# A two-part transformer kernel on one core: another order in its opening stage, context rows scaled on GpSimd, and waits for a quarter of a weight unit

## The chip, the cores and the metric

The kernel runs on 1 core of one Trainium2 chip. The metric is device time in microseconds (us), lower is better. TensorE does the matrix products, VectorE (DVE), ScalarE (ACT) and GpSimd (POOL) the element-wise work, SyncE (SP) issues most transfers.

## The reference

512 tokens `x` and 256 context tokens `ctx`, both 1024 wide, pass through two modulated layers, and `x` then through a larger block. For this change it is enough to see how a layer begins:

```python
mod_x = (silu_c @ w_mod[i] + b_mod[i])[:, None, :]
mod_c = silu_cc @ w_mod[i] + b_mod[i]
sh_x, sc_x, g_x = jnp.split(mod_x, 3, axis=-1)
sh_c, sc_c, g_c = jnp.split(mod_c, 3, axis=-1)
hx = rms_norm(x, norm_g[i]) * (1.0 + sc_x) + sh_x
hc = rms_norm(ctx, norm_g[i]) * (1.0 + sc_c) + sh_c
# layer 0 (a): grouped attention with rotary positions over x and ctx
q, k, v, z = cut(hx @ w_in); kc, vc = cut(hc @ w_in)   # and qc, zc
...
# layer 1 (b): attention in a neighbourhood, and to the context
```

So nothing of a layer can be projected before its row norms and its modulation vectors (shift, scale and gate, each 1024 wide, for `x` and for `ctx`) are there. All data are float32.

## The kernel before

**Layout.** Tokens lie along the free dimension, features over the 128 partitions in 8 chunks k. `XX` holds x (8 x 512 columns), `XC` the context (8 x 256). A float32 product is made of three matmuls on parts in a shorter format: high part `WH` by high part `HX`, `WH` by the rest `LX` of the activations, rest `WL` of the weights by `HX` (L1267 to L1269; L1262 to L1264 where tokens are the stationary side; `HC` and `LC` are the context's parts).

**Weights** come in 1 MB units (`UNITS`), 128 x 2048 each, two buffers deep (`load`). A unit is split into its parts in four quarters of 512 columns: ScalarE casts a quarter to `WH` (L1549), then GpSimd, or VectorE for the first two units and in `flush`, subtracts it to `WL` (L2255, L1800). `tick` puts the next quarter into the plan, between chunks of projections. Chunk k of a unit lies in quarter k // 2. `proj` waits at k = 0 for all four quarters (L1254, L1255).

**Modulation units** are split in nothing: 16 small matmuls (`mod_mm`, L1280), ScalarE copies the sums to a row (`mod_row`, L1556), TensorE turns it into columns (`mod_tr`, L1289), VectorE adds the bias (L1806). Unit i of a layer holds shift (i from 0 to 3), scale (4 to 7) or gate (8 to 11) of chunks 2i and 2i + 1, modulo 8. Six of layer 0's units (`EARLY`) have buffers of their own, four of them; units 2 and 6 come through the ordinary stream.

**Opening stage.** First loads: vectors, x in two halves, context, then early units on SP's queue; the constants `C` and the rotary table `CS` on ScalarE's queue. Squares of x and ctx, added up chunk by chunk (L1566, L1568, L1814), column sums on TensorE (`norm_sums`, L1298), the power -1/2 on GpSimd (`norm_rs`, L2261), and six diagonal products that spread it over PSUM (`rbroad`, L1305). Then `modulate` per chunk k: VectorE multiplies x by gain and norm (`scale`, L1856), ScalarE adds the shift and casts to `HX` (L1576), VectorE makes the rest `LX` (`scale_low`, L1863); the context part of the chunk the same way just behind, on the same engines. `keys_rows` projects the keys of chunk k as chunks come free. Next come the values (`values`), the norm and rotation of the keys (`a_key_sums`, `a_key_norm`, `a_key_rope`), the first pair of queries (`gen_aq(0)`: `a_query_raw`, `a_query_sums`, `a_query_rope`), and the first scores of attention (L1347).

**Order.** The program is one list (`plan`) that each engine walks in the order in which `do` was called, taking the steps that it has a part in. An engine that waits in a step holds up all its later steps. Banks of PSUM are given out by rings.

Of the kernel before, what the change touches and what calls it, by code (L numbers as in the profile page):

```python
# [74 lines left out]
EARLY = [0, 4, 1, 5, 3, 7]  # L75
# [91 lines left out]
def build(nc, wu, vp, cc, cs1, xt, biasb, pos, out):  # L167
    ctx = ExitStack()
    with ctx:
# [81 lines left out]
        s_gain, s_scaled, s_res = signal("mod_gain"), signal("scaled"), signal("residual")  # L251
        s_r2 = signal("norm2")
# [161 lines left out]
        def early_load(n):  # L414
            do("early", n)

        def early_unit(n, nxt=None):
            w = early[n % 4].rearrange("p (k f) -> p k f", k=8)
            run(mod_unit(0, EARLY[n], MODS, w, (s_early[n % 4], (n,)), lambda: early_load(nxt) if nxt else None))

# [36 lines left out]

        part_by = {}
        scaled = {}

        def modulate(l, Rb, rb, perm, hb, phase, first):
            a = smc(16).rearrange("p (f j) -> p f j", j=2)
            scaled[l] = (a, Rb, rb, perm, hb, phase, first)
            for k in range(KC):
                do("scale", l, k)
                for j in range(2):
                    part_by[phase, k, j] = "dve"
                if k:
                    do("scale_low", l, k - 1)
                if k == KC - 1:  # L470
                    do("scale_low", l, k)
                yield k
# [7 lines left out]
        partsrc = {}  # L480
        WIDE = ring((0, 1), (2, 3), (4, 5), (6, 7))
# [9 lines left out]
        mod = [smc(48).rearrange("p (f j) -> p f j", j=2) for _ in range(2)]  # L491
        do("first_loads")
# [7 lines left out]
        do("silu")  # L500
        for n in range(2):
            split(n)
        ar = Arena()
        hb0 = Rows(ar(4096), ar(2048))
        norm("a", ar, 6, (), lambda k: [(s_x[k // 4], (k // 4,)), (s_x[2], (2,))])
        for k in range(KC):
            do("square", "a", k)
        early_unit(0, 4)
        early_unit(1, 5)
        close("a", MODS)  # L510
        WIDE.take("RA", (s_scaled, (0, 7, 1)))
        RbA = PS[:, 0:1024]
        rbroad("a", 6, RbA)
        mods = modulate(0, RbA, "a", False, hb0, "a", ())
        next(mods), next(mods)
        un = Unit("ak")

# [7 lines left out]
        early_unit(2)  # L525
        early_unit(3)
        keys_rows([0])
# [3 lines left out]
        keys_rows([1, 2])  # L531
        unv = Unit("av")
        run(mod_units(0, (2,), MODS))
        run(mod_units(0, (6,), MODS))
        next(mods), next(mods)
        keys_rows([3, 4])
        early_unit(4)
        early_unit(5)
        next(mods), next(mods)
        keys_rows([5, 6, 7])  # L540
# [12 lines left out]
        ksq, krr = [tmpS, PbA[0]], [PTbA[0], PTbA[1]]  # L553
        kss = smc(24)
# [9 lines left out]
        values((0, 1))  # L564
        do("a_key_sums")
        values((2, 3))
        for m in range(2):
            do("a_key_norm", m)
        values((4,))
        for m in range(2):  # L570
            do("a_key_rope", m)
        values((5,))
        unv.done(s_proj, "av", 5)
        for b in range(4, 8):
            last[b] = [(s_ksin, ((b - 4) // 2,))]

# [185 lines left out]
        run(gen_aq(0, FA))  # L762
# [45 lines left out]
        b0 = WIDE.take("RB", (s_scaled, (1, 7, 1)))  # L808
# [17 lines left out]

        def b_free(a):

            return [(s_post, ("b", 8 * (a - 2) + 7))] if a >= 2 else [(s_xl_dve, ("b", 7, 1))]
# [419 lines left out]
        def tensor(e, w):  # L1249
            def proj(g, k):  # L1250
                G = groups[g]
                if k == 0:
                    free(w, g)
                    for q in range(4):  # L1254
                        w.wait_ge(*w_low(G.unit, q))  # L1255
# [36 lines left out]
            def norm_sums(name):  # L1292
# [3 lines left out]
                w.wait_ge(*s_acc(name, 7))  # L1296
# [31 lines left out]
            def a_query_sums(pair):  # L1328
                free(w, ("aqs", pair))
                w.wait_ge(*s_qsq(pair, 1))  # L1330
                for i in range(6):
                    t = e.matmul(aqps[pair, "sums"][:, 2 * i:2 * i + 2], tmpS[:, i * 128:i * 128 + 128], c("ind"), start=True, stop=True)
# [52 lines left out]
            def m_gates():  # L1385
                free(w, "gw")
                for q in range(4):
                    w.wait_ge(*w_low(gwu, q))
                part = PART[gwu]
                for k in range(8):  # L1390
                    w.wait_ge(*x_low("h", k, 0))
# [140 lines left out]
        def scalar(e, w):  # L1532
            def first_loads():
                e.dma_start(C[:, :], cc).then_inc(*s_c.by())

            def rope_load():
                e.dma_start(CS[:, :], cs1).then_inc(*s_cs.by())

# [18 lines left out]

            def square(name, k):
# [11 lines left out]

            def scale(l, k):
                a, Rb, rb, perm, hb, phase, first = scaled[l]
                for j, (lo, hi) in enumerate(FULL):
                    w.wait_ge(*s_scaled(l, k, j))
                    await_all(w, first)
                    e.activation(H.at(k, lo, hi), hb.at(k, lo, hi), ACT.Identity, bias=mod[l][:, k, j:j + 1]).then_inc(*s_xh.by(phase, k, j))  # L1576
# [7 lines left out]
            def a_key_raw(m):  # L1584
                w.wait_ge(*s_proj("ak", 1, 1))
                w.wait_ge(*s_xl_dve("a", 7, 1))
# [9 lines left out]
            def a_query_raw(pair, j):  # L1596
                lo, hi = FULL[j]
                w.wait_ge(*s_proj("aq", pair, j))
                await_all(w, [(s_qrope, (pair - 1,))] if pair else [(s_krope, (0,)), (s_krope, (1,))])
                e.activation(tmpS[:, lo:hi], groups["aq", pair, j].out[:, 0:hi - lo], ACT.Square).then_inc(*s_qsq.by(pair, j))  # L1600
# [972 lines left out]
```

## Time and profile before

| | |
|---|---|
| median of 3 runs | 1780.09 us (1779.31 to 1780.92) |
| the profiled execution | 1784.24 us, its span 1782.5 us |
| TensorE busy | 1607.6 us, 90% |
| VectorE, ScalarE, GpSimd busy | 732.4, 611.6, 606.9 us |
| granted TensorE clock, mean | 0.941 of full speed |

Busy time is the sum of instructions' durations. Rows of a timeline begin with start and duration (us), and in brackets at the end the engine's idle time before the instruction and what ended it. In the rows PE is TensorE's matmuls and PEld its weight loads.

### The profile page before, as it was taken

To read this page: it belongs to the slowest core of one execution; us is meant where nothing else is said; L and a number is where in the kernel's file an instruction comes from. 1 tells how busy PE (TensorE), PEld (TensorE's weight loads), DVE (VectorE), ACT (ScalarE), POOL (GpSimd) and SP (SyncE) were. 2 spreads that over 40 slices of the span, in tenths; PEclk is the share of its full clock that TensorE was granted. 3 is DMA by queue.
4 is the path that set the end of the run, shared out by engine and by line. 5 is a ranking of instruction groups with operands and counts; after the bars stand their busy time and mean duration, and the time that the engine had idled before them with its cause. 6 is when DMAs were issued, how large, how long until landed. Compare 5 with 4: busy or idle time off the path is not lost.

```text
span 1782.5 us, 25034 instructions
## 1 busy us (share of the span) xinstructions
PE 1607.6 (90%) x9858; PEld 1255.4 (70%) x9858; DVE 732.4 (41%) x1730; ACT 611.6 (34%) x1289; POOL 606.9 (34%) x590
## 2 busy tenths in 40 slices
PE   3799999999869799999997879999999888999987
PEld 2577777777648688788876658778787775555756
DVE  3434444444442524345355452514332354554033
ACT  3224444434432323333334342424332233333221
POOL 0033334333222124243333443435345233332351
PEclk9789999999969899999999989999999899999998
DMA  7201011111222222121221202122121211111221
GB/s 309 80 24 48 35 41 49 44 48 49 87 101 92 100 72 83 65 87 57 89 71 48 95 30 94 48 71 79 63 94 48 95 71 43 53 48 48 71 89 53
DMA packets 22148, 128.21 MB, mean 72 GB/s; under 512 B 2448, under 2 KB 2576, under 8 KB 8080
## 3 DMA queue, kind: packets, MB, share of 16 engines
q1 hardware_dynamic: 21600, 125.03, 19.5%
q8 instruction: 79, 1.29, 0.3%
q10 hardware_dynamic: 432, 1.58, 0.2%
q14 instruction: 37, 0.30, 0.0%
HBM read 124.50 MB, written 2.10 MB: 71 GB/s over the span
## 4 chain that ended last, share of the span: by engine, by line
PE 75%; DVE 10%; issue 5%; POOL 4%; ACT 4%; DMA 2%; SPq 0%; DVEq 0%; POOLq 0%; ACTq 0%
PE PS L1267 14%; PE PS L1268 13%; PE PS L1269 13%; PE PS L1347 6%; PE PS L1382 6%; PE PS L1357 5%; PE PS L1513 3%; PE PS L1262 2%; PE PS L1263 2%; PE PS L1264 2%; POOL WL L2255 2%; DVE sm L1940 1%; PE PS L1523 1%; DVE AR L2054 1%; DVE AR L1856 1%
## 5 line engine op out<-in xcount | busy, mean ns | idle before, releaser
L2255 POOL TENSOR_TENSOR WL<-W,WH 128x512 fp32r<-128x512 f32 x268 | 348.0, 1313 | 475.9 <-ACT WH L1549 475.4
L1267 PE MATMUL PS<-HX,WH 128*128 128x512 f32 x1008 | 421.1, 418 | 38.4 <-POOL WL L2255 18.3
L1268 PE MATMUL PS<-LX,WH 128*128 128x512 f32 x1008 | 403.8, 401 | 0.0
L1269 PE MATMUL PS<-HX,WL 128*128 128x512 f32 x1008 | 403.4, 400 | 0.0
L1267 PEld LDWEIGHTS PS<-HX,WH 128*128 128x128 f32 x1008 | 196.5, 195 | 88.8 <-issue 30.5
L1269 PEld LDWEIGHTS PS<-HX,WL 128*128 128x128 f32 x1008 | 195.5, 194 | 43.3
L1268 PEld LDWEIGHTS PS<-LX,WH 128*128 128x128 f32 x1008 | 196.6, 195 | 37.3 <-issue 1.7
L1549 ACT CAST WH<-W 128x512 fp32r<-128x512 f32 x296 | 170.8, 616 | 42.0 <-DMA W<-in_wu 34.7
L1618 ACT ACTIVATE AR<-PS,sm 128x768 f32<-128x768 f32 (+4 forms) x160 | 115.5, 722 | 182.5 <-DVE sm L1945 105.3
L1940 DVE TENSOR_REDUCE sm<-PS 128x1 f32<-128x512 f32 (+4 forms) x224 | 149.9, 669 | 43.7 <-PE PS L1347 39.3
L2298 POOL TENSOR_SCALAR AR<-AR,sm 128x768 f32<-128x768 f32 (+1 forms) x96 | 73.3, 763 | 231.3 <-DVE sm L1956 231.3
L1347 PE MATMUL PS<-AR 64*128 64x256 f32 (+3 forms) x704 | 128.1, 472 | 13.7 <-ACT XC L1618 5.2
L1382 PE MATMUL PS<-AR 128*64 128x128 f32 x1408 | 102.6, 294 | 20.7 <-DVE AR L1965 12.0
L1382 PEld LDWEIGHTS PS<-AR 128*64 128x64 f32 x1408 | 81.8, 145 | 49.1 <-issue 31.0
L1347 PEld LDWEIGHTS PS<-AR 64*128 64x128 f32 x704 | 61.5, 191 | 68.4 <-issue 45.8
L1262 PE MATMUL PS<-WH,HX 128*128 128x256 f32 x320 | 95.6, 299 | 14.7 <-POOL WL L2255 14.7
L1357 PE MATMUL PS<-C,AR 128*128 128x128 f32 x608 | 103.9, 291 | 4.4 <-DVE AR L1976 4.1
L1628 ACT COPY AR<-PS 128x512 f32<-128x512 f32 (+1 forms) x112 | 62.1, 554 | 126.4 <-PE PS L1357 125.9
L2298 POOL TENSOR_SCALAR XC<-XC,sm 128x512 f32<-128x512 f32 x64 | 44.7, 698 | 162.9 <-DVE sm L1956 162.9
L1357 PEld LDWEIGHTS PS<-C,AR 128*128 128x128 f32 x608 | 71.3, 146 | 40.6 <-issue 25.4
L1618 ACT ACTIVATE XC<-PS,sm 128x512 f32<-128x512 f32 x64 | 44.1, 690 | 150.6 <-DVE sm L1945 150.6
L1263 PE MATMUL PS<-WH,LX 128*128 128x256 f32 x320 | 93.3, 292 | 0.0
(266 smaller groups left out, 2467.7 us busy)
## 6 DMA issues: line engine op xcount, KB each, us to landing
W<-in_wu SPq DMA_DIRECT2D x100, 1024.0 KB, 4.8
AR<-in_biasb SPq DMA_DIRECT2D x32, 256.0 KB, 2.6
AR<-in_wu SPq DMA_DIRECT2D x6, 1024.0 KB, 15.4
XX<-in_xt SPq DMA_DIRECT2D x2, 1024.0 KB, 9.7
out<-XX SPq DMA_DIRECT2D x8, 256.0 KB, 2.2
XC<-in_xt SPq DMA_DIRECT2D x1, 1024.0 KB, 12.7
C<-in_cc ACTq DMA_DIRECT2D x1, 770.5 KB, 5.3
CS<-in_cs ACTq DMA_DIRECT2D x1, 512.0 KB, 8.8
```

The source lines that it names most:

```text
L1262: e.matmul(o, xh, wh, start=(k == 0), stop=False)
L1263: e.matmul(o, xl, wh, start=False, stop=False)
L1267: e.matmul(o, wh, xh, start=(k == 0), stop=False)
L1268: e.matmul(o, wh, xl, start=False, stop=False)
L1269: t = e.matmul(o, wl, xh, start=False, stop=(k == 7))
L1347: t = e.matmul(PS[:, s.score[h] + a:s.score[h] + b], l, r, start=True, stop=True)
L1357: t = e.transpose(o[:, j * 128:j * 128 + 128], s.pb[h][:, (q0 + j) * 128:(q0 + j) * 128 + 128], c("id"))
L1382: t = e.matmul(s.out[h], s.values[h][j], s.pt[h][:, j * 128:j * 128 + 128], start=(j == 0 and s.first), stop=(j == nv - 1 and s.final))
L1549: e.copy(WH[:, PART[n], a:z], W[:, n % 2, a:z]).then_inc(*s_wh.by(n, q))
L1618: e.activation(s.pb[h][:, 0:s.n], PS[:, s.score[h]:s.score[h] + s.n], ACT.Exp, bias=smn[:, i % 4:i % 4 + 1], scale=(1.0 if s.scale is None ...
L1940: e.tensor_reduce(mx, x, AX.X, ALU.max).then_inc(*s_max.by(name, n, h))
L2255: e.tensor_tensor(WL[:, d, a:z], W[:, n % 2, a:z], WH[:, d, a:z].bitcast(F32), ALU.subtract).then_inc(*s_wl_pool.by(n, q))
```

## The change

In the opening stage:

- The constants go onto SP's queue behind the context, and the rotary table behind the second weight unit. All eight shift and scale units of layer 0 are `EARLY` ones (units 2 and 6 leave the stream); units 4 to 7 of them wait in SP's queue for the four buffers.
- The squares are made and added for x first, by halves as they land, then for the context.
- `norm_sums` goes between the first and the second `mod_mm`, the first `mod_tr` behind the second, the second behind `rbroad`. Later modulation units go in pairs, both `mod_mm` ahead of both `mod_tr`, with a chunk of key projections between.
- The first query pair is projected between the values, with a scratch tile of its own.

In both layers' `modulate` the context's part moves: ScalarE copies the context's norms to SBUF (`Rc`), GpSimd multiplies all eight chunks by them, then per chunk multiplies by the gain and adds the shift; ScalarE only casts, and GpSimd makes the rest `LC`.

In the whole kernel `proj` waits for quarter k // 2 at chunk k in place of all four at k = 0, and `m_gates` likewise. Waits for the last context part go to GpSimd's signal (`H_A`, `H_B`).

```diff
-    u = [("ak",), ("av",), ("mod", 0, 2), ("mod", 0, 6), ("aqz", 0)]
+    u = [("ak",), ("av",), ("aqz", 0)]
-EARLY = [0, 4, 1, 5, 3, 7]
+EARLY = [0, 4, 1, 5, 2, 6, 3, 7]
...
         def modulate(l, Rb, rb, perm, hb, phase, first):
+            do("scale_ctx", l)
             for k in range(KC):
                 do("scale", l, k)
-                for j in range(2):
-                    part_by[phase, k, j] = "dve"
+                part_by[phase, k, 0], part_by[phase, k, 1] = "dve", "pool"
...
         do("first_loads")
-        for n in range(2):
-            early_load(n)
+        do("early", range(4))
         load(0)
-        for n in range(2, 4):
-            early_load(n)
+        do("early", range(4, 8))
         load(1)
         do("rope_load")
         do("silu")
...
+        for j in range(2):
+            for k in range(KC):
+                do("square_part", "a", k, j)
+        first = [early_unit(n, FIRST if n < 4 else MODS) for n in range(8)]
+        next(first[0])
+        norm_sums("a", FIRST)
+        next(first[1])
+        run(first[0])
+        do("norm_rs", "a")
...
+        rbroad("a", 6, RbA)
+        run(first[1])
+        for n in range(2):
+            split(n)
         mods = modulate(0, RbA, "a", False, hb0, "a", ())
-        next(mods), next(mods)
+        next(mods)
         un = Unit("ak")
+        next(mods)
+        next(first[2])
+        next(first[3])
+        run(first[2])
+        run(first[3])
...
+        for n in (4, 6):
+            next(mods), next(mods)
+            keys_rows([n - 4])
+            next(first[n])
+            next(first[n + 1])
+            keys_rows([n - 3])
+            run(first[n])
+            run(first[n + 1])
         next(mods), next(mods)
         while pieces:
             tick()
         unv = Unit("av")
-        keys_rows([5, 6, 7])
+        keys_rows([4, 5, 6, 7])
...
-        run(gen_aq(0, FA))
+        aq0 = gen_aq(0, vr)
...
+        values((0, 1))
+        key_work[0]()
+        values((2,))
+        key_work[1]()
+        to_pause(aq0), to_pause(aq0)
+        key_work[2]()
+        values((3,))
+        to_pause(aq0)
+        values((4,))
+        run(aq0)
+        values((5,))
...
# TensorE, proj
                 if k == 0:
                     free(w, g)
-                    for q in range(4):
-                        w.wait_ge(*w_low(G.unit, q))
+                w.wait_ge(*w_low(G.unit, k // 2))
...
# ScalarE
+            def scale_ctx(l):
...
+                w.wait_ge(*s_rb(rb, 5))
...
+                e.copy(Rc, Rb[:, T:NT]).then_inc(*s_rc.by(l))
             def scale(l, k):
+                w.wait_ge(*s_scaled(l, k))
+                e.activation(H.at(k, 0, T), hb.at(k, 0, T), ACT.Identity, bias=mod[l][:, k, 0:1]).then_inc(*s_xh.by(phase, k, 0))
+                w.wait_ge(*s_scaled_ctx(l, k))
+                e.copy(H.at(k, T, NT), hb.at(k, T, NT)).then_inc(*s_xh.by(phase, k, 1))
...
# GpSimd
+            def scale_ctx(l):
+                w.wait_ge(*s_rc(l))
...
+                for k in range(KC):
+                    e.tensor_tensor(hb.at(k, T, NT), xT.at(k, T, NT), Rc, ALU.mult).then_inc(*s_normed_ctx.by(l, k))
+            def scale(l, k):
...
+                w.wait_ge(*s_gain(l, k | 1))
+                w.wait_ge(*s_normed_ctx(l, k))
+                e.tensor_scalar(hb.at(k, T, NT), hb.at(k, T, NT), a[:, k, 1:2], mod[l][:, k, 1:2], ALU.mult, ALU.add).then_inc(*s_scaled_ctx.by(l, k))
+            def scale_low(l, k):
...
+                w.wait_ge(*s_xh(phase, k, 1))
+                e.tensor_tensor(L.at(k, T, NT), hb.at(k, T, NT), H.at(k, T, NT).bitcast(F32), ALU.subtract).then_inc(*s_xl_pool.by(phase, k, 1))
...
# SyncE
+                e.dma_start(C[:, :], cc).then_inc(*s_c.by())
...
+            def early_(ns):
+                for n in ns:
+                    if n >= 4:
+                        w.wait_ge(*s_modmm(0, EARLY[n - 4]))
+                    e.dma_start(early[n % 4], wu[len(UNITS) + n]).then_inc(*s_early[n % 4].by(n))
```

The comment lines that name an engine are added here. `key_work` is the list of `a_key_sums`, `a_key_norm` and `a_key_rope`; `to_pause` runs the query generator to its next pause: x's projection, the context's, `a_query_sums`, then `a_query_rope` with the rest.

## Rows read from the trace of the kernel before

**Rows 1.** Busy time by stretch: length, then each engine, granted clock, DMA share, GB/s

```profile
0.00:45.06 45.06, 16.77 (x104) 11.21 (x105) 14.97 (x30) 14.27 (x30) 1.86 (x7) 0.95 0.78 310
45.06:88.50 43.44, 33.06 (x177) 24.72 (x178) 18.29 (x41) 10.29 (x20) 0.00 (x0) 0.70 0.21 77
88.50:130.20 41.70, 37.96 (x284) 33.89 (x283) 12.97 (x20) 13.54 (x19) 17.76 (x11) 0.90 0.07 26
130.20:136.00 5.80, 5.79 (x15) 3.61 (x16) 2.41 (x5) 1.58 (x3) 0.23 (x1) 0.51 0.01 3
...
606.50:632.50 26.00, 18.22 (x72) 14.35 (x73) 23.45 (x43) 11.64 (x21) 0.00 (x0) 0.86 0.15 53
```

**Rows 2.** Waits of TensorE: total us, times, longest

```profile
PE PS L1267 <- POOL WL L2255: 18.3, 10, 4.1
PE PS L1262 <- POOL WL L2255: 14.7, 5, 5.5
```

**Rows 3.** Timeline of the opening stage, TensorE

```profile
17.38 1.93 PE L1280 MATMUL PS<-AR,sm 128*32 128x256 f32 x16 [17.38 <-DMA AR<-in_wu]
...
27.58 2.70 PE L1298 MATMUL PS<-C,AR 128*128 128x1 f32 x12
32.33 2.93 PE L1305 MATMUL PS<-AR,C 128*128 128x128 f32 x12 [2.05 <-DVE AR L1836]
...
40.79 0.98 PE L1289 MATMUL PS<-C,AR 128*128 128x2 f32 x4 [3.71 <-ACT AR L1556]
...
45.06 0.77 PE L1267 MATMUL PS<-HX,WH 128*128 128x512 f32 x1
...
130.21 2.93 PE L1347 MATMUL PS<-AR 64*128 64x512 f32 x8 [3.10 <-DVE AR L1914]
```

**Rows 4.** Timeline of the opening stage, ScalarE and VectorE

```profile
14.93 0.63 ACT L1566 ACTIVATE AR<-XX 128x512 f32<-128x512 f32 x1 [9.30 <-DMA XC<-in_xt]
...
16.72 7.33 DVE L1814 TENSOR_TENSOR AR<-AR 128x768 f32<-128x768 f32 x7 [10.88 <-ACT AR L1568]
...
38.22 2.16 ACT L1549 CAST WH<-W 128x512 fp32r<-128x512 f32 x4
```

**Rows 5.** Busy time by stretch, the transfers at full rate (last column GB/s)

```profile
10.00:20.00 10.00, 1.93 (x16) 0.59 (x16) 2.96 (x4) 4.62 (x11) 0.00 (x0) 1.00 1.01 423
```

**Rows 6.** Groups by shape, GpSimd: count, busy us, mean ns, idle before

```profile
L2272 POOL TENSOR_TENSOR LC<-AR,HC 128x256 fp32r<-128x256 f32 x4 | 4.2, 1056 | 0.0
L2298 POOL TENSOR_SCALAR AR<-AR,sm 128x256 f32<-128x256 f32 x32 | 15.3, 478 | 54.1 <-DVE sm L1956 54.1
L2276 POOL TENSOR_TENSOR sm<-sm 128x24 f32<-128x24 f32 x1 | 4.2, 4162 | 3.9 <-DVE sm L1882 3.9
```

**Rows 7.** Busy time by stretch: key projections first, then a stretch of values, then queries

```profile
45.06:50.33 5.27, 5.27 (x17) 4.40 (x17) 4.80 (x11) 2.65 (x5) 0.00 (x0) 0.50 0.08 33
...
98.40:101.50 3.10, 3.10 (x17) 3.10 (x16) 0.32 (x1) 0.00 (x0) 3.10 (x2) 0.50 0.00 0
115.00:120.40 5.40, 5.40 (x24) 4.46 (x25) 0.86 (x2) 5.30 (x8) 0.00 (x0) 1.00 0.00 0
```

**Rows 8.** Timeline: three of TensorE's 15 waits for quarters, and one pair of quarters

```profile
930.43 0.47 PE L1267 MATMUL PS<-HX,WH 128*128 128x512 f32 x1 [4.09 <-POOL WL L2255]
...
1065.80 2.56 POOL L2255 TENSOR_TENSOR WL<-W,WH 128x512 fp32r<-128x512 f32 x2 [6.44 <-ACT WH L1549]
...
1068.50 0.55 PE L1262 MATMUL PS<-WH,HX 128*128 128x256 f32 x1 [5.52 <-POOL WL L2255]
...
1719.64 0.72 PE L1267 MATMUL PS<-HX,WH 128*128 128x512 f32 x1 [2.89 <-POOL WL L2255]
```

**Rows 9.** Timeline, GpSimd and VectorE at work on SBUF together

```profile
111.11 2.53 POOL L2281 TENSOR_TENSOR AR<-AR,CS 128x512 f32<-128x512 f32 x2 [7.15 <-PE PS L1326]
...
112.50 1.70 DVE L1894 TENSOR_TENSOR AR<-AR 128x512 f32<-128x512 f32 x1 [0.74 <-POOL AR L2281]
114.83 0.69 DVE L1894 TENSOR_TENSOR AR<-AR 128x512 f32<-128x512 f32 x1
```

More of the change, by code:

```diff
@@ L412, in mod_units, with early_unit @@
                 yield from mod_unit(l, u, pr, unit_w(un.n), (s_w[un.n % 2], (un.n,)), lambda: un.done(s_modmm, l, u))
-        def early_load(n):
-            do("early", n)
-        def early_unit(n, nxt=None):
+        def early_unit(n, pr):
             w = early[n % 4].rearrange("p (k f) -> p k f", k=8)
-            run(mod_unit(0, EARLY[n], MODS, w, (s_early[n % 4], (n,)), lambda: early_load(nxt) if nxt else None))
+            return mod_unit(0, EARLY[n], pr, w, (s_early[n % 4], (n,)), lambda: None)
         @dataclass
@@ L500, in build @@
         do("silu")
+        ar = Arena()
+        hb0 = Rows(ar(4096), ar(2048))
+        norm("a", ar, 6, (), None)
+        for j in range(2):
[7 more added lines that the diff above has]
+        do("norm_rs", "a")
+        WIDE.take("RA", (s_scaled, (0, 7)), (s_rc, (0,)))
+        RbA = PS[:, 0:1024]
+        rbroad("a", 6, RbA)
+        run(first[1])
         for n in range(2):
             split(n)
[L503 to L513, printed above, removed]
         mods = modulate(0, RbA, "a", False, hb0, "a", ())
-        next(mods), next(mods)
+        next(mods)
         un = Unit("ak")
+        next(mods)
[3 more added lines that the diff above has]
+        run(first[3])
         def keys_rows(ks):
@@ L553, in build @@
         ksq, krr = [tmpS, PbA[0]], [PTbA[0], PTbA[1]]
+        qtmp = [PbA[1] if pair == 0 else tmpS for pair in range(8)]
         kss = smc(24)
@@ L563, in values @@
                 do("a_value", s)
[L564 to L573, printed above, removed]
         for b in range(4, 8):
             last[b] = [(s_ksin, ((b - 4) // 2,))]
+        key_work = [lambda: do("a_key_sums"), lambda: [do("a_key_norm", m) for m in range(2)], lambda: [do("a_key_rope", m) for m in range(2)]]
         @dataclass
@@ L761, in fill_a, with to_pause @@
             yield from parts_a(range(7))
-        run(gen_aq(0, FA))
+        aq0 = gen_aq(0, vr)
+        def to_pause(g):
+            while next(g) != PAUSE:
+                pass
+        values((0, 1))
[9 more added lines that the diff above has]
+        values((5,))
+        unv.done(s_proj, "av", 5)
         attention("a", [s for pair in range(8) for s in steps_a(pair)], SA, TA, PbA, PTbA, OA, fill_a(), 8 * 15 * (T + LC) / 100 + 14 * 5, posted_a)
@@ L807, in build @@
         close("b", ONE)
-        b0 = WIDE.take("RB", (s_scaled, (1, 7, 1)))
+        b0 = WIDE.take("RB", (s_scaled, (1, 7)), (s_rc, (1,)))
         RbB = PS[:, 512 * b0:512 * b0 + 1024]
@@ L1295, in norm_sums @@
                 w.wait_ge(*s_c())
-                w.wait_ge(*s_acc(name, 7))
+                await_all(w, [(s_acc, (name, 7, j)) for j in range(2)] if name == "a" else [(s_acc, (name, 7))])
                 for i in range(N.nt):
@@ L1331, in a_query_sums @@
                 for i in range(6):
-                    t = e.matmul(aqps[pair, "sums"][:, 2 * i:2 * i + 2], tmpS[:, i * 128:i * 128 + 128], c("ind"), start=True, stop=True)
+                    t = e.matmul(aqps[pair, "sums"][:, 2 * i:2 * i + 2], qtmp[pair][:, i * 128:i * 128 + 128], c("ind"), start=True, stop=True)
                 t.then_inc(*s_qsum.by(pair))
@@ L1386, in m_gates @@
                 free(w, "gw")
-                for q in range(4):
-                    w.wait_ge(*w_low(gwu, q))
                 part = PART[gwu]
                 for k in range(8):
+                    w.wait_ge(*w_low(gwu, k // 2))
                     w.wait_ge(*x_low("h", k, 0))
@@ L1556, in mod_row, with square_part @@
                 e.copy(mrow[b], modps[l, u][0][:, 0:256]).then_inc(*s_mrow.by(l, u))
+            def square_part(name, k, j):
+                N, (lo, hi) = norms[name], FULL[j]
+                w.wait_ge(*(s_x[2](2) if j else s_x[k // 4](k // 4)))
+                if k > 2:
+                    w.wait_ge(*s_acc(name, k - 2, j))
+                o = N.acc if k == 0 else N.sq[(k - 1) % 2]
+                e.activation(o[:, lo:hi], xT.at(k, lo, hi), ACT.Square).then_inc(*s_sq.by(name, k, j))
             def square(name, k):
```

93 lines of the change are left out of this document (44 added, 49 removed).

## The prediction

> **What bounds the kernel now.** I read the stretches first. TensorE is busy nine tenths of the span, so a gain must come out of its idle or slow time. From the start to the first key projection it works 16.77 of 45.06 us; through keys and modulation units 33.06 of 43.44, at a mean granted clock of 0.70; through values and first queries 37.96 of 41.70; and the first attention steps run at 0.51 [rows 1]. So 130 us of opening hold some 42 us without a matmul, and a good part of the rest runs at 1.2 GHz. Then the waits of TensorE: the largest that recur after the opening are for GpSimd's quarters, 18.3 and 14.7 us [rows 2]; by the timeline all 15 lie between 848 and 1735 us. The timeline of the opening shows what is late at each point: the first modulation unit lands at 17.38, the norm sums run only at 27.58, the spread at 32.33, the first key row at 45.06, the first scores at 130.21 [rows 3].
>
> **Part 1, up to the norms.** Squares began at 14.93, on the context's landing, because every chunk took x and context together; the adds ran from 16.72 for 7.33 us [rows 4]. Transfers move 423 GB/s [rows 5]. By that landing vectors 0.24 MB, x 2.10, context 1.05, constants 0.79 and table 0.52 had been asked for, 4.70 MB in all. In the new order x's first half needs 1.29 MB, (4.70 - 1.29) / 0.423 = 8 us earlier, at 7; the context 3.39 MB, at 11.8; the first early unit 5.23 MB in place of 5.75, 1.2 us earlier, at 16.2. Most adds now hide under the transfers; only the context's, a third of the columns, 7.33 / 3 = 2.4 us and some latency, come behind the last: done about 16.3. TensorE: `mod_mm` 16.2 to 18.1 (1.93), sums to 20.9 (2.70), second `mod_mm` to 22.8, first `mod_tr` to 23.8 (0.98). VectorE takes that turned column ahead of the norm, so the 2.05 us chain to the spread starts at 23.9, not at 20.9: spread from 26.0 to 28.9 (2.93), before to 35.3. The second `mod_tr` and its gain stand behind it: first scaled chunk at 30.6.
>
> **Part 2, the context on GpSimd, first layer.** This is the new wait. ScalarE's list is now: cast of x chunk 0, cast of context chunk 0, four casts of the key weights, chunk 1, `mod_row` of the third and fourth unit. The context cast waits for GpSimd, which does eight multiplies first. No such multiply is in the trace; the nearest rows are 1.056 us for a 128x256 subtract that ran beside VectorE, and 0.478 for a one-input 128x256 operation [rows 6]. Bounds for eight: 3.8 and 8.4 us. I take 0.7 each, as half of the 1.28 us that 128x512 takes [rows 8] with something for the start: 5.6 us. From 29.4: 35.1, gain 35.6, cast 36.0, weight casts 38.2 (2.16 [rows 4]), chunk 1 to 40.7, `mod_row` pair 41.4. Then two `mod_tr` to about 43.2, and the first key row: 1.9 us earlier than 45.06, of the 6.3 won before. Bounds: 41 to 46.
>
> **Part 3, keys to first scores.** The work between is the same: eight key chunks, four modulation units. Before, TensorE stopped at each pair of units until their gain had been applied, and each stop was followed by a stretch at half clock, such as 45.06 to 50.33 at 0.50 [rows 7]. Now a chunk that is ready stands behind each pair of `mod_mm`, and a pair of `mod_tr` in front of chunks whose gain is two pairs old, so I find no stop longer than 1 us. At full clock a key chunk has 4608 columns; 24 matmuls of 512 took 5.40 us at clock 1.00 [rows 7], so 2.0 us, 16.2 for eight. Units: half the slow 1.93 and 0.98 [rows 3], 1.5 each, 5.8 for four. One slow start of 5.27 us does half its work: 2.6 more. Sum 24.6, and 2 for short waits: keys end at 70, before at 88.5. The stretch to the scores loses its 41.70 - 37.96 = 3.7 us idle, because values cover the query's chain, and gains a stop: the key power takes 4.16 us on GpSimd [rows 6], and only one value tile (24 matmuls of 256 columns, 2.9 us) now covers it, so with latency 1.6. 41.7 - 3.7 + 1.6 = 39.6: first scores at 109.6 for 130.2, 20.6 us less. Coming from work, not from idleness, the first 5.8 us of attention need not run at 0.51: 2.7 less. The second query unit's quarters, formerly split before attention, are now split inside it: 1 more. Sum of the opening: -22; bounds -12 (key rows at 46, and two more slow stretches of 5.3) and -27.
> Transfers do not bind here: units 4 to 7 wait in SP's queue for `mod_mm`; behind them queue the value weights and the table, asked for at about 34, wanted at 64 and 95.
>
> **Part 4, quarters.** A quarter takes GpSimd 1.28 us [rows 8]; a 512-wide group works 1.37 us on it, a token-wide one 0.7. So a wait for the last of four can shrink by up to 4.1 us, and disappears where the earlier quarters lie ready. Case by case: at 1068.50 the last two quarters came at 1065.80 to 1068.36, so two quarters' work goes ahead and the end moves 2.2 us of the 5.52; the chain to that pair starts in set-up work on VectorE, so the 2.2 us won just before (1049.55) is lost in it. At 930.43 only 2 of the 4.09 remain, since the next transposes wait for softmax work that TensorE does not hold up. 1719.64 keeps its 2.9 [rows 8]. The other eleven, done the same way, give 13 to 15. Sum -22; as some will be handed to the next wait, I take -17, bounds -8 and -24. The added waits sit inside the stream of matmuls; the existing wait per chunk for `LX` shows no gap where it is already met, so I cost them at nothing.
>
> **Part 5, second layer's modulation.** There VectorE is busy 23.45 of 26.00 us [rows 1] and sets the pace. It gives up the context, about a third of its work, but its weight quarters and all later chunks now stand behind ScalarE's first context cast, which waits for GpSimd's eight multiplies: 6 us lost, 6 to 7 won. I take +1, from -2 to +6.
>
> The rule that speaks against the change: in the trace a VectorE add with two SBUF inputs took 1.70 us while GpSimd worked on SBUF and 0.69 alone [rows 9]. The Trainium skill, SBUF — State Buffer, section Who interferes with whom, says that such a pair shares a read interface and that the later one is blocked for the whole of the earlier. The trace agrees: the 1.70 us end 0.56 us after GpSimd's second operation. By the rule the total below could rise to 1750, by the undisturbed row it stays at 1742; the third rival works it out from rows.
>
> **The sum.** -22 - 17 + 1 = -38 against the profiled 1784.24 us: 1746.2. The median of the runs is 4.15 us under that execution, so 1742.
>
> **Rivals.** *Quarters give little*: attention and the recurrent stage follow chains on ScalarE and VectorE, and TensorE only waits elsewhere. For it: the 930 and 1049 cases. Against: most chains begin with TensorE's own projections and move with it. Part 4 at -4: 1755.
> *The opening gives half*: GpSimd's multiplies take 1.06 us, key rows start at 46, and the clock falls again around each pair of units, as at 98.40 [rows 7]. All of the opening at -11: 1753.
> *VectorE and GpSimd shut each other out*: in the second layer 12 two-input VectorE operations each wait up to 0.7 us for one of GpSimd's 24: at most 8 more, 1750 with all; in the first layer the key rows hide it. For it: the slow add of [rows 9]. Against: chunks come 1.7 us apart, so most pairs need not meet.
> *Slower*: one mechanism, ScalarE in order behind GpSimd's 24 context operations per layer. Each 0.8 us beyond my price, over 48 operations, costs the 38 us; so it decides from about 1.5 us per operation, against a largest row of 1.06. Then all else is used up, and with 1.7 us it is 1790.
> *The change does nothing*: only if the transfers of the first 16 us, now on one queue, slow down; by the sizes, after 14.93 only SP's queue had transfers left, and the rate over that stretch was the full one [rows 5]. I count it with the second.
>
> **Chances.** Forecast 0.55, quarters 0.17, opening 0.13, shut out 0.10, slower 0.05. Its own range is 1732 to 1751 (opening -27 to -18, quarters -22 to -12); with the rivals 1726 to 1760. A measurement of this kernel tells 0.2%, 3.6 us, from no change: faster 0.94, same 0.02, slower 0.04.
>
> **What would show it.** Norm sums at 18 to 21 us; GpSimd's eight multiplies from 29 to 35 with ScalarE idle beside them; key rows at 43; clock near full from 49 on; first scores at 107 to 112; TensorE's waits for quarters down from 33 us to under 15; second layer's modulation as long as before. It is wrong if the clock falls between the unit pairs, if a context operation takes over 1 us, or if the quarters' stops come back as waits for VectorE.

## The result, and the profile after

The changed kernel takes 1724.99 us (median of 4 runs, 1720.54 to 1725.59) beside 1779.7 for the kernel before (4 runs, 1778.88 to 1780.92): ratio 0.9687, interval 0.9669 to 0.9704, so 54.7 us less where 37.7 were forecast (1779.7 to 1742). The time lies 1 us under the range. Its profiled execution took 1725.52 us, span 1723.7; the span before was 1782.5. The spans differ by 58.8, since the profiled execution of before was 4 us over its median.

How much earlier TensorE reaches the same work, from the two timelines:

| TensorE starts | before | after | earlier by |
|---|---|---|---|
| first norm's sums | 27.58 | 17.36 | 10.2 |
| first key row | 45.06 | 42.29 | 2.8 |
| first scores | 130.21 | 108.87 | 21.3 |
| second step of scores | 143.64 | 119.61 | 24.0 |
| output projection of layer 0 | 522.99 | 496.69 | 26.3 |
| second norm's sums | 600.00 | 572.70 | 27.3 |
| end of layer 1's modulation | 632.56 | 607.87 | 24.7 |
| third norm's sums | 1013.81 | 981.59 | 32.2 |
| recurrent heads 0, 1, 2, 3 | 1082.85, 1156.26, 1234.66, 1308.33 | 1047.15, 1118.38, 1189.56, 1261.12 | 35.7, 37.9, 45.1, 47.2 |
| last attention's projections | 1443.05 | 1389.06 | 54.0 |
| final norm's sums | 1769.60 | 1710.77 | 58.8 |

24 us come from the opening, as forecast (22). The rest is won in steps that sit where the stops for quarters were, and lost in one place only, layer 1's modulation.

Busy time by stretch of the changed kernel: up to the first key row, to the last keys, to the first scores, the first attention steps, and layer 1's modulation behind the spread (answering to [rows 1]; same columns):

```profile
0.00:42.29 42.29, 14.85 (x105) 10.95 (x105) 15.68 (x35) 15.19 (x31) 9.15 (x18) 0.92 0.94 381
42.29:71.60 29.31, 26.67 (x178) 21.24 (x179) 15.99 (x27) 9.48 (x20) 9.94 (x13) 0.88 0.11 42
71.60:108.87 37.27, 36.71 (x282) 33.70 (x281) 12.93 (x20) 12.49 (x17) 15.27 (x9) 0.95 0.08 29
108.87:114.87 6.00, 6.00 (x28) 4.41 (x29) 2.58 (x6) 3.13 (x6) 1.58 (x2) 1.00 0.01 3
579.17:607.87 28.70, 18.56 (x74) 14.88 (x74) 17.93 (x27) 11.20 (x22) 17.56 (x24) 0.72 0.19 63
```

The key stretch shrank from 43.44 to 29.31 us, its clock rose from 0.70 to 0.88, and the first attention steps start at full clock. In the last line VectorE has 5.5 us less to do than before, yet the stretch is 2.7 us longer.

Waits of TensorE in the changed kernel (answering to [rows 2]):

```profile
PE PS L1304 <- ACT AR L1564: 18.6, 9, 9.6
...
PE PS L1282 <- DVE LX L1891: 10.6, 4, 4.7
...
PE PS L1277 <- POOL WL L2283: 2.5, 5, 1.1
PE PS L1282 <- POOL LC L2312: 2.2, 1, 2.2
```

Another 1.3 us at L1282 are for GpSimd's quarters, so 3.8 are left of 33.0. What leads now is a wait for ScalarE's row copies, 9.6 us of it in one piece. The timelines of the opening show what that is, TensorE first (answering to [rows 3]), then ScalarE, then GpSimd:

```profile
15.50 1.93 PE L1295 MATMUL PS<-AR,sm 128*32 128x256 f32 x16 [15.50 <-DMA AR<-in_wu]
17.36 2.72 PE L1313 MATMUL PS<-C,AR 128*128 128x1 f32 x12
...
25.01 2.93 PE L1320 MATMUL PS<-AR,C 128*128 128x128 f32 x12 [2.12 <-DVE AR L1867]
...
40.19 1.84 PE L1304 MATMUL PS<-C,AR 128*128 128x2 f32 x8 [9.57 <-ACT AR L1564]
42.29 0.80 PE L1282 MATMUL PS<-HX,WH 128*128 128x512 f32 x1 [0.25 <-DVE sm L1829]
...
108.87 1.56 PE L1362 MATMUL PS<-AR 64*128 64x512 f32 x8 [0.52 <-DVE AR L1906]
```

```profile
30.68 0.72 ACT L1597 ACTIVATE HX<-AR,sm 128x512 fp32r<-128x512 f32 x1 [2.33 <-DVE AR L1886]
34.51 0.40 ACT L1599 CAST HC<-AR 128x256 fp32r<-128x256 f32 x1 [3.11 <-POOL AR L2307]
34.82 2.17 ACT L1557 CAST WH<-W 128x512 fp32r<-128x512 f32 x4
...
39.69 0.64 ACT L1564 COPY AR<-PS 128x256 f32<-128x256 f32 x2
```

```profile
28.43 5.51 POOL L2301 TENSOR_TENSOR AR<-XC,AR 128x256 f32<-128x256 f32 x8 [3.79 <-ACT AR L1591]
```

GpSimd multiplies all eight context chunks in 5.51 us. ScalarE waits for it at 34.51 with the key weights' casts, the second chunk and the two row copies queued behind, and TensorE idles 9.57 us for those copies. This is the wait that the forecast placed in its second part, with nearly its numbers.

### The profile page after: what moved, and what is told of

The parts are those of the page before. It is cut to its first block, busy times and chain, and to the rows that moved or that the text cites. A ratio compares the mean times of both kernels' runs of the same rounds, so it can differ in the third digit from the quotient of the medians.

```text
span 1723.7 us, 24997 instructions
## 1 busy us (share of the span) xinstructions
PE 1588.2 (92%) x9858; PEld 1246.0 (72%) x9858; DVE 728.0 (42%) x1705; ACT 610.4 (35%) x1291; POOL 642.9 (37%) x638
## 4 chain that ended last, share of the span: by engine, by line
PE 80%; DVE 7%; issue 5%; POOL 3%; ACT 3%; DMA 1%; SPq 0%; POOLq 0%; DVEq 0%; ACTq 0%
PE PS L1282 14%; PE PS L1283 14%; PE PS L1284 14%; PE PS L1362 6%; PE PS L1397 6%; PE PS L1372 5%; PE PS L1527 3%; PE PS L1277 3%; PE PS L1279 3%; PE PS L1278 3%; DVE sm L1968 1%; PE PS L1537 1%; POOL WL L2283 1%; DVE AR L2082 1%; PE PS L1450 1%
## 5 line engine op out<-in xcount | busy, mean ns | idle before, releaser
L1282 PE MATMUL PS<-HX,WH 128*128 128x512 f32 x1008 | 414.0, 411 | 14.1 <-DVE LX L1891 10.6
L1283 PE MATMUL PS<-LX,WH 128*128 128x512 f32 x1008 | 398.3, 395 | 0.0
L1284 PE MATMUL PS<-HX,WL 128*128 128x512 f32 x1008 | 398.2, 395 | 0.0
L1282 PEld LDWEIGHTS PS<-HX,WH 128*128 128x128 f32 x1008 | 192.8, 191 | 60.0 <-issue 15.1
L1283 PEld LDWEIGHTS PS<-LX,WH 128*128 128x128 f32 x1008 | 192.7, 191 | 36.4 <-issue 1.9
L1557 ACT CAST WH<-W 128x512 fp32r<-128x512 f32 x296 | 171.0, 617 | 43.2 <-DMA W<-in_wu 35.9
L1279 PE MATMUL PS<-WL,HX 128*128 128x256 f32 x320 | 93.4, 292 | 0.0
```

The source lines that it names most:

```text
L1279: t = e.matmul(o, xh, wl, start=False, stop=(k == 7))
L1282: e.matmul(o, wh, xh, start=(k == 0), stop=False)
L1283: e.matmul(o, wh, xl, start=False, stop=False)
L1284: t = e.matmul(o, wl, xh, start=False, stop=(k == 7))
L1557: e.copy(WH[:, PART[n], a:z], W[:, n % 2, a:z]).then_inc(*s_wh.by(n, q))
```

## The experiments

Each ratio is to runs of the kernel before on the same chip. The runs stand in four groups, each with its own runs of the kernel before: the first four edits (its median 1777.25 us), the changed kernel again with the next three (1780.4), columns first to the first filled stops (1778.83), and the last two (1776.53). Where runs of two groups are compared, the difference of their ratios stands beside that of the times; 0.001 of a ratio is 1.8 us. The changed kernel itself was timed a second time, beside three of the runs below:

> The changed kernel itself, beside the next three on the same chip: 1725 us if this chip is like the first; its ratio to the kernel before stays at 0.969.

It gave 1724.07 us (1720.16 to 1725.76), ratio 0.968 (0.9658 to 0.9702).

**The quarters alone.** The kernel before with one edit (and the same in `m_gates`):

```diff
                 if k == 0:
                     free(w, g)
-                    for q in range(4):
-                        w.wait_ge(*w_low(G.unit, q))
+                w.wait_ge(*w_low(G.unit, k // 2))
```

> The kernel before, with nothing of the change but the wait for each quarter of a unit where it is used. Theory: the quarters are worth some 35 us, twice what the forecast took (17), because they also remove the stop for a unit split by VectorE (5.05 us at 523) and the half-clock matmuls that follow a stop: 1745 us (1740 to 1750), and the opening up to the first scores stays within 2 us of 130. Rival: the quarters give the 17 to 22 us that the forecast worked out, and the surplus comes from the new opening carrying through the later stages: 1758 to 1763.

1744.27 us beside 1777.25 (ratio 0.9816, 0.98 to 0.9831): 33.0 less. The forecast's 17 is refuted, whatever the opening does.

**The rest without the quarters.** The changed kernel with the edit the other way round:

> The changed kernel, with its waits for quarters put back to all four ahead of a group's first matmul (gates too). Theory: 35 us come back and the opening keeps its gain: 1760 us (1755 to 1764); the stops of the trace of before return at the same places (before head 1's and head 3's work, at the start of the second attention), each followed by matmuls at half clock. Rival: only the 17 to 22 us of the forecast come back: 1742 to 1748.

1760.69 us (ratio 0.9907, 0.9892 to 0.9921), some 36 more than the changed kernel (39 to 40 by the ratios). The stops came back at the old places but one (1158.91), and there is a new one, at the second query unit, whose quarters are now split inside attention. The waits for quarters, then that stop:

```profile
PE PS L1283 <- POOL WL L2285: 20.5, 10, 4.1
...
PE PS L1278 <- POOL WL L2285: 14.7, 5, 5.5
...
PE PS L1283 <- DVE WL L1825: 3.2, 1, 3.2
```

```profile
122.83 0.77 PE L1283 MATMUL PS<-HX,WH 128*128 128x512 f32 x1 [3.63 <-POOL WL L2285]
```

So the two halves of the change help each other: the opening alone gives 16.6 us (1777.25 to 1760.69), the quarters alone 33.0, both 54.7. The 5 that the sum lacks belong to the stop that the new opening would make at that unit and the waits per quarter take away: at 149 us, behind it, this run is 5.2 us later than the second execution of the changed kernel, and at 96 us it was 1.2 us ahead, so 6.4 us go across that stop.

**Only GpSimd's quarters ahead.**

```diff
+                    for q in range(4):
+                        if split_by[G.unit, q] == "pool":
+                            w.wait_ge(*w_low(G.unit, q))
                 w.wait_ge(*w_low(G.unit, k // 2))
```

> As the run with all quarters first, but only quarters that GpSimd makes are waited for ahead of the first matmul; those that VectorE makes are waited for where they are used. Theory: VectorE's quarters are 4 to 5 us of the 35 (the stop at 523): 1755 us, 4 to 5 less than with all quarters first. Rival: only GpSimd's waits matter, as the forecast counted: within 1 us of the run with all quarters first.

1760.55 us (ratio 0.9913, 0.9892 to 0.9935). The time did not move, but the stop did: the idle time ahead of layer 0's output projection shrank from 3.21 us to 1.31, and across it this run gains 2 us on the run with all quarters first. It was 1.3 us behind at 498 us, having lost up to 2.1 within the first attention, where the programs are the same; it is 0.8 ahead at 502 us and still 0.6 at the end. So the stop pays about 2 of the theory's 4 to 5 us, and the medians do not resolve them.

**The first layer's context back on VectorE and ScalarE** (`scale_ctx` left out for layer 0, the second operation per chunk as in the kernel before):

> The changed kernel, with the context of the first layer's modulation scaled on VectorE and cast with its shift on ScalarE, as before; the second layer's stays on GpSimd. Theory: GpSimd's eight multiplies stood in front of ScalarE's list (TensorE idle 9.57 us ahead of the third unit's columns), so the first key row comes 4 us earlier than 42.3 and the total is 1721 us. Rival: VectorE then has some 2.3 us of work per chunk against TensorE's 2.0 and becomes the bound of the keys: what is won at the first row is lost by the eighth, 1725 to 1729.

1721.22 us (ratio 0.9685, 0.9668 to 0.9702): by the ratio no different from the changed kernel. The trace shows both theories at work: first key row at 38.67, 3.6 us earlier, then waits for VectorE between the last key rows (1.77 us, 0.55 us), first scores at 107.08, 1.8 earlier.

**The second layer's context back on VectorE and ScalarE** (the same edit for layer 1):

> The changed kernel, with the context of the second layer's modulation back on VectorE and ScalarE as before; the first layer's stays on GpSimd. Theory: GpSimd's eight multiplies at the head of ScalarE's list cost that stage 2.6 us (it took 35.17 us against 32.56 before), which come back: 2 to 3 us less than the changed kernel. Rival (the forecast's: 6 lost and 6 to 7 won): VectorE is the pace there, and with the context back on it the stage is as long or longer: 0 to 4 us more than the changed kernel.

1721.5 us (ratio 0.967, 0.965 to 0.9691) beside 1724.07: 2.6 less. The intervals overlap, but from the second norm's sums to the first attention step behind that stage the trace is 2.5 us shorter than the changed kernel's. This agrees with the theory; the difference is about what the runs can resolve.

**A multiply per chunk on GpSimd**, both layers:

```diff
 def scale_ctx(l):
...
-    for k in range(KC):
-        e.tensor_tensor(hb.at(k, T, NT), xT.at(k, T, NT), Rc, ALU.mult).then_inc(*s_normed_ctx.by(l, k))
 def scale(l, k):
...
+    e.tensor_tensor(hb.at(k, T, NT), xT.at(k, T, NT), Rc, ALU.mult).then_inc(*s_normed_ctx.by(l, k))
     w.wait_ge(*s_gain(l, k | 1))
```

> The changed kernel, but GpSimd multiplies each context chunk just before it applies that chunk's gain, in place of all eight ahead of the first; both layers. Theory: the eight multiplies were what held ScalarE, so its first context cast comes 4 us earlier than at 34.5, the first key row at 38.5 for 42.3, and the second layer's modulation is 2 to 4 us shorter: 1718 us, 6 to 8 less than the changed kernel. Rival: GpSimd then sets the pace of the chunks with some 1.8 us each and shuts VectorE out of the SBUF in the middle of its chain, and what is won at the first row is gone at the eighth: within 2 us of the changed kernel.

1717.37 us (ratio 0.9644, 0.9623 to 0.9666), 6.7 less than the changed kernel. ScalarE and TensorE of this run:

```profile
30.36 0.72 ACT L1597 ACTIVATE HX<-AR,sm 128x512 fp32r<-128x512 f32 x1 [1.84 <-DVE AR L1886]
30.99 0.39 ACT L1599 CAST HC<-AR 128x256 fp32r<-128x256 f32 x1
31.29 2.17 ACT L1557 CAST WH<-W 128x512 fp32r<-128x512 f32 x4
```

```profile
37.27 1.84 PE L1304 MATMUL PS<-C,AR 128*128 128x2 f32 x8 [5.58 <-ACT AR L1564]
39.36 0.79 PE L1282 MATMUL PS<-HX,WH 128*128 128x512 f32 x1 [0.26 <-DVE sm L1829]
```

The context cast follows its neighbour with no wait at all, 3.5 us earlier than in the changed kernel, and TensorE's idle time falls from 9.57 to 5.58. So it was the eight multiplies ahead of the first gain, not the move to GpSimd, that held ScalarE. About half of the gain is the second layer's: from the second norm's sums to the first attention step behind that stage 62.83 us pass, for 66.30 in the second execution of the changed kernel.

**Rows first**: `next(first[2])` and `next(first[3])` moved ahead of the first chunk's scaling, on top of the last:

> As the run with a multiply per chunk, and the third and fourth modulation unit's matmuls and ScalarE's copies of their rows stand ahead of the first chunk's scaling. Theory: the two rows are then turned before the key weights are cast, TensorE's wait for them (9.57 us) falls under 3 us, and the first key row comes at 36 for 38.5 without this step: 2 us less than the run with a multiply per chunk, 1716 us. Rival: the first key row waits for the casts of the key weights, which the copies only push back: no difference, or 1 us more.

1713.58 us (ratio 0.9629, 0.9606 to 0.9653), 3.8 less than without this step, with intervals that overlap. First scores at 104.74, for 106.90 without this step. The first key row gained only 0.6 us (38.78): it now waited 5.47 us for VectorE's add of the turned columns, which stood behind the split of the key weights.

**Columns first**, on top of that:

```diff
         next(mods)
-        un.append(Unit("ak"))
-        next(mods)
         run(first[2])
         run(first[3])
+        next(mods)
+        un.append(Unit("ak"))
```

> As the run with a multiply per chunk and rows first; besides, VectorE adds the two turned columns right behind the first chunk's scaling, and the key weights are split only behind the second chunk's. In that run the first key row waited 5.47 us for VectorE's add, which stood behind the split of the key weights. Theory: the first key row comes at 36.5 for 38.8, the first scores at 102.5 for 104.7, and the total is 1711.5 us, 2 less. Rival: the weights' casts are then 1.5 us later and the first key row waits for these in place of the add: within 1 us.

1712.64 us (1710.05 to 1714.29; ratio 0.9631, 0.9616 to 0.9646). The shortest median, 12 us under the changed kernel's (9 to 10 by the ratios), but by the ratio no different from the run with rows first. The trace moved more than the time: first key row at 34.66, first scores at 100.83, 3.9 us earlier than in the last run. Whether those 3.9 us reach the end, the times of two groups do not tell.

**Squares that wait for the context**, as in the kernel before; the order of the loads stays:

```diff
-                w.wait_ge(*(s_x[2](2) if j else s_x[k // 4](k // 4)))
+                w.wait_ge(*s_x[k // 4](k // 4))
+                w.wait_ge(*s_x[2](2))
```

> The changed kernel, but every square waits for the context too, as in the kernel before; the order of the loads stays. Theory (the forecast's first part): the squares then start at 11.8 for 7 and end some 4 us later, the norm's sums come at 21 for 17.4, and all behind them by as much: 1728 us. Rival: the early units' landing at 15.5 and ScalarE's and GpSimd's work behind the norm set the first key row anyway: within 1 us of the changed kernel.

1728.05 us (ratio 0.972, 0.9705 to 0.9734). Norm's sums at 21.66, 4.3 us later, first key row at 46.55, 4.3 later, 3 to 4 in the total (6 to 7 by the ratios). The early squares carry through to the end.

**Keys behind all units**, in place of between them:

```diff
             next(mods), next(mods)
-            keys_rows([n - 4])
             next(first[n])
             next(first[n + 1])
-            keys_rows([n - 3])
             run(first[n])
             run(first[n + 1])
...
-        keys_rows([4, 5, 6, 7])
+        keys_rows(range(8))
```

> The changed kernel, but all eight key chunks stand behind the last modulation unit, in place of between the units. Theory: TensorE stops again at each pair of units (3 to 4 us) and starts the keys at half clock, so the keys end 6 to 8 us later: 1732 us. Rival: what sets the end of the keys is VectorE's chain of chunks, which starts its later chunks sooner when the units come first: keys end within 2 us of 71.6, the total within 2 us of the changed kernel or below it.

1725.02 us (ratio 0.9702, 0.9687 to 0.9718): the changed kernel's time, or 3 to 4 us more by the ratios, whose intervals overlap. The theory's 1732 is out, and the keys end at 73.4 us, within 2 us of 71.6, as the rival said. TensorE of this run:

```profile
46.86 1.05 PE L1302 MATMUL PS<-C,AR 128*128 128x2 f32 x8 [1.04 <-ACT AR L1562]
47.84 1.93 PE L1293 MATMUL PS<-AR,sm 128*32 128x256 f32 x32
52.52 1.49 PE L1302 MATMUL PS<-C,AR 128*128 128x2 f32 x8 [2.75 <-ACT AR L1562]
53.88 0.77 PE L1280 MATMUL PS<-HX,WH 128*128 128x512 f32 x1
```

The stops are there, 1.04 and 2.75 us, and the first row starts 11.6 us later, yet the first scores come at 110.85, close behind the changed kernel's two executions (108.87, 110.35). With the units early, every chunk is scaled when its turn comes: from 60 to 75 us TensorE works without a gap at full clock, where the changed kernel worked 13.17 us at 0.89.

**Stops filled.** All quarters first, as above, but with extra matmuls in 13 of the stops:

```diff
+                    if g in FILL:
+                        w.wait_ge(*x_low(G.phase, 0, 0))
+                        for _ in range(FILL[g]):
+                            e.matmul(G.out[:, 0:256 if G.by_tokens else 512], H.at(0, 0, 128), H.at(0, 0, 256 if G.by_tokens else 512), start=True, stop=True)
                     for q in range(4):
                         w.wait_ge(*w_low(G.unit, q))
```

> The run with all quarters ahead of the first matmul, but in 13 of its stops TensorE does extra matmuls on data that is there (their sums are overwritten by the group's own first matmul), almost as long as the stop was. The stops stay, only the idleness in them goes. Theory: some 11 of the 35 us that the quarters are worth are the half clock after a stop, so these come back: 1750 us (1747 to 1754) for 1760.7, with the matmuls after the stops at full pace. Rival: the clock has no part, the stops' length is the whole price: 1760 to 1764, since an extra matmul can only lengthen a stop.

1758.42 us (ratio 0.989, 0.9872 to 0.9909). The theory of 11 us fell, but some fillers outlasted their stop, so a second run has fewer:

> The run with filled stops again, with fewer extra matmuls in four of the stops (28 for 40, 10 for 17, 6 for 12, 10 for 11), where they had outlasted the stop by about 1 us each. Theory: the clock behind a stop is a small part of the 35 us, 2 to 5: 1755 to 1758 us. Rivals: it is the 11 us of the first reckoning, hidden by the outlasting: 1750; or nothing: 1760 and more.

1756.53 us (ratio 0.9885, 0.9868 to 0.9901): 4 us less than with the stops left empty, though the two intervals still overlap a little. What the clock won was mostly given back. At ten of the stops the first filled run gains 0.9 to 2.5 us on the unfilled one, some 16 together, and it loses most of that again between them: it was 4.8 us ahead of the unfilled one at head 1 and 1.6 us a little later; in between, at 1134.60, it waited 1.55 us for a unit's quarters, a stop that the unfilled run had not.

**Waits per half of a unit:**

```diff
-                w.wait_ge(*w_low(G.unit, k // 2))
+                if k in (0, 4):
+                    for q in range(2):
+                        w.wait_ge(*w_low(G.unit, k // 2 + q))
```

> The changed kernel, with the first two quarters of a unit waited for ahead of the first matmul and the last two ahead of the fifth chunk. Theory: each stop shrinks by the work that goes ahead of the last wait, or by all of itself if that is less, and nothing is handed on. Over the 16 stops of the run with all quarters first, with 1.37 us of work per quarter in a 512-wide group and 0.7 in a token-wide one, that is 33.3 us with quarters (35.7 measured) and 27.1 with halves: 6 us more than the changed kernel, 1731 (1729 to 1733). Rival (the forecast's): a part of each gain is handed to the next wait, and half of the difference with it: 1728. Second rival: it is the whole unit that comes late or early, and halves do as well as quarters: 1725 to 1726.

1731.04 us (1727.45 to 1732.32; ratio 0.9738, 0.9721 to 0.9755), 6 to 7 us over the two medians of the changed kernel (9 to 10 by the ratios). The intervals exclude that halves do as well; the second rival is out. The first one (1728, 3 us over) lies inside the spread of the runs, but the ratios speak against it. The stops that are left:

```profile
PE PS L1279 <- POOL WL L2285: 6.4, 4, 2.5
PE PS L1284 <- POOL WL L2285: 4.2, 3, 2.2
```

## Why the prediction was right in direction and wrong in size

**Part 1 held.** Forecast: sums 18.1 to 20.9, spread at 26.0; sums began at 17.36, the spread at 25.01. Undoing the early squares alone costs 4.3 us at the first key row, near the 4.8 between the part's landings of x's first half and of the context (7 and 11.8).

**Part 2 held.** Forecast: multiplies 5.6 us, first key row at 43.2; measured 5.51 and 42.29. The head of ScalarE's list was the price, and the multiply per chunk shows that the move did not need it.

**Part 3 held in its sum, and in part for another reason.** Keys end at 71.6 (70), first scores at 108.87 (109.6), and attention starts at full clock. But the part put the gain down to key chunks that stand between the unit pairs. With the chunks moved behind the units the time is the same, or 3 to 4 us longer by ratios whose intervals overlap, so no run shows that the interleaving itself gave anything. What paid is then the earlier start and that most chunks find their gain and their split weights ready; that is argued, and how much is due to each is open, so that the sum came out is partly luck. The part also found no stop longer than 1 us. One of 1.83 us, for VectorE, came behind the last pair of units and one of 0.81 behind it, and then the granted clock was 0.50 for 3 us (timeline, then busy time of the stretch):

```profile
61.02 0.50 PE L1282 MATMUL PS<-HX,WH 128*128 128x512 f32 x1 [1.83 <-DVE LX L1891]
...
62.79 0.54 PE L1282 MATMUL PS<-HX,WH 128*128 128x512 f32 x1 [0.81 <-DVE LX L1891]
```

```profile
63.13:66.12 2.99, 2.99 (x10) 2.53 (x9) 1.92 (x3) 0.59 (x2) 0.77 (x1) 0.50 0.01 5
```

**Part 5 held within its bounds.** Forecast +1 (-2 to +6); measured +2.7 in the stretch, and 2.6 less when the context goes back. With a multiply per chunk, still on GpSimd, that stage is 3.5 shorter, so the row of eight multiplies cost it more than the move won. The rival of engines that shut each other out is seen, and it is small:

```profile
38.65 0.74 DVE L1891 SCALAR_TENSOR_TENSOR LX<-AR,sm,HX 128x512 fp32r<-128x512 f32 x1
...
43.40 1.21 DVE L1891 SCALAR_TENSOR_TENSOR LX<-AR,sm,HX 128x512 fp32r<-128x512 f32 x1
```

The same VectorE operation of the changed kernel takes 0.74 us alone and 1.21 beside GpSimd's subtract of 43.33, 0.47 more. The Trainium skill, SBUF — State Buffer, section Who interferes with whom, has the later of such a pair blocked for the whole of the earlier, here the 0.66 us that the subtract still had to run; the trace agrees that it waits, but for 0.47 only. In the second layer's modulation the eight operations of this kind took 6.64 us together, 0.7 more than eight alone.

**Part 4 is the step that failed, by its size.** It took 17 us, and the quarters alone gave 33.0; the gap of 16 is nearly the whole miss (1742 to 1725). Its rule was sound: a stop can shrink by up to three quarters' work, 4.1 us in a 512-wide group, 2.1 in a token-wide one, or by all of itself if that is less. Applied to the 15 stops of [rows 2] without further thought, it gives 28.0. What went wrong came after, in three places:

- "The other eleven, done the same way, give 13 to 15", and 1049.55 and 930.43 reduced by hand: 28 became 22, on the ground that another wait would end as late. Then 5 more were taken off for gains "handed to the next wait". Laid side by side, the timelines of the kernel before and of the run with the quarters alone show how much the second gains across each stop: 6.0 us at 930.43 for the 2 taken (the wait of 4.09, and 1.7 in the matmuls behind it), 3.6 for the 2.2 at 1049.55 and 1068.50 together, 4.7 for the 2.9 at 1719.64, and about 19 for the 13 to 15 of the other eleven. These two executions differ by 40 us in all, where the medians differ by 33, so the sizes are rough, but the 5 appear nowhere. Only the reduction at 1049.55 proved right: the 4 us won there are gone again just ahead of 1068.50. Halving the grain costs 6 to 7 us, 9 to 10 by the ratios, where the plain rule says 6.2.
- The list held only stops that name GpSimd. VectorE's quarters at 522.99 stopped TensorE 5.05 us in the kernel before:

```profile
522.99 0.76 PE L1267 MATMUL PS<-HX,WH 128*128 128x512 f32 x1 [5.05 <-DVE WL L1800]
```

  By the rule that is 4.1 more, 32.2 in all, against 33.0 measured, but so close a sum is partly luck. A stop can also shrink no further than the time by which the first part comes ahead of the last, and VectorE makes four quarters in 2.50 us, so here that is 1.9. In the run with the quarters alone:

```profile
516.76 2.50 DVE L1798 TENSOR_TENSOR WL<-W,WH 128x512 fp32r<-128x512 f32 x4 [1.96 <-ACT WH L1547]
...
517.55 0.77 PE L1266 MATMUL PS<-HX,WH 128*128 128x512 f32 x1 [2.96 <-issue]
```

  It was 3.3 us ahead of the kernel before at 515.20, is 5.4 ahead at 522.99 and 6.0 at 533.02. The changed kernel gains as much here on the run with all quarters first, 2.6 and 2.7 us in its two executions. So this stop pays some 2 to 3 us; with 1.9 for it the rule gives about 30.
- The half clock behind a stop was counted in the opening only. Filled stops bring 2 to 4 us of the 36 to the end, much less than the 11 of the first reckoning, and near what the runs can resolve; most of what they win at the stops is lost again on the way.

Head 2 shows stop and clock together, before (1156.26 to 1234.66) and after:

```profile
1156.26:1234.66 78.40, 73.55 (x368) 60.74 (x367) 27.92 (x45) 27.55 (x48) 33.18 (x30) 0.96 0.19 68
```

```profile
1118.38:1189.56 71.18, 70.51 (x367) 58.40 (x367) 28.85 (x48) 27.57 (x48) 33.69 (x30) 1.00 0.20 75
```

7.2 us, of which 3.0 are busy time at a clock of 0.96 for 1.00. Why the gains were handed on so seldom is argued, not shown: behind most stops lie projections whose other operands had long been there, and ScalarE's casts for the next unit stand in a list that itself follows TensorE, so the quarters came earlier together with their users.

## What to carry to other kernels

Where an engine stops for the last of several parts, take the stop's whole length, up to the work that the earlier parts allow and the time by which they come ahead of the last, and take something off only where the trace names the wait that ends as late; sum the stops by the kind of the wait, not by the engine that causes most of them. Before moving work to an idle engine, order it there by first need: eight operations ahead of the first result held two other engines for 3 to 4 us, one operation at a time for 0.6 us at most. And try the interleaving that costs trouble against the plain order, since the plain order may do as well.

## What the runs showed of the hardware that was not expected

GpSimd's 128x256 multiply took 0.69 us in the row of eight and 1.17 beside VectorE's split of the key weights (32.23 us in the run with a multiply per chunk), and VectorE's four operations of that split took 3.21 us there for 2.61 in the changed kernel: both engines pay for a meeting.

Two executions of the changed kernel differ by 2.8 us within the first attention, at the same program and in the same stretch. Busy time of 360 to 440 us, the first execution and the second:

```profile
360.00:380.00 20.00, 18.38 (x157) 14.22 (x154) 9.80 (x28) 10.18 (x22) 8.87 (x8) 0.91 0.00 1
...
400.00:420.00 20.00, 18.26 (x147) 14.87 (x147) 8.78 (x23) 8.14 (x17) 5.02 (x6) 0.95 0.01 2
420.00:440.00 20.00, 19.03 (x141) 13.97 (x140) 7.68 (x24) 4.87 (x14) 5.43 (x6) 0.88 0.15 53
```

```profile
360.00:380.00 20.00, 18.39 (x181) 14.36 (x179) 10.70 (x30) 10.17 (x22) 8.88 (x8) 1.00 0.00 1
...
400.00:420.00 20.00, 18.26 (x153) 14.47 (x153) 8.80 (x24) 8.45 (x17) 5.73 (x7) 1.00 0.01 2
420.00:440.00 20.00, 18.99 (x147) 14.57 (x148) 8.90 (x26) 5.90 (x15) 5.03 (x6) 0.92 0.15 53
```

The granted clock was 0.91, 0.95 and 0.88 in the one and 1.00, 1.00 and 0.92 in the other. So a landmark of two profiles that differs by under 3 us says nothing of a change, unless it differs at one place only, where the change is.
